# Nine products of ones ahead of the first panels, input tiles in another order, three subtractions moved to VectorE, a copy moved ahead of an exponential, and the last square added by TensorE

## The reference

```
h = rmsnorm(x, norm_attn)
proj = h @ w_in          # queries, keys, values, gates of both mixers
o_nsa = gates over (compressed, selected, sliding-window) attention, 8 heads
o_sb  = stick-breaking attention, 8 heads
mixed = sigmoid(g0) * (o_nsa @ w_up_nsa) + sigmoid(g1) * (o_sb @ w_up_sb)
x = x + mixed @ w_out
x = x + square(relu(rmsnorm(x, norm_mlp) @ w_ff1)) @ w_ff2
return rmsnorm(x, norm_final)
```

## Time and profile before

| | |
|---|---|
| median of 3 runs | 813.46 us (813.44 to 814.03) |
| the profiled execution | 813.46 us, of which the span from first to last instruction is 811.7 us |
| TensorE busy | 786.6 us, 97% of the span |
| VectorE, ScalarE, GpSimd busy | 442.3, 328.7, 283.3 us |
| HBM traffic | 73.90 MB read, 2.13 MB written |

### The profile page before, as it was taken

One profiled execution on the slowest core, in us unless ns is written; L12 is line 12 of the kernel. 1 busy time (PEld: TensorE's weight loads), 2 busy tenths in 40 slices (PEclk: granted clock), 3 DMA queues, 4 the chain that ended last, 5 costly groups with the idle time before them and its releaser, 6 DMA issues.

```text
span 811.7 us, 11300 instructions
## 1 busy us (share of the span) xinstructions
PE 786.6 (97%) x3984; PEld 642.6 (79%) x3984; DVE 442.3 (54%) x780; ACT 328.7 (41%) x583; POOL 283.3 (35%) x123
## 2 busy tenths in 40 slices
PE   6999999999999999999999999999999999999995
PEld 4878988878767677668888888888888888888895
DVE  6545346766646666745736287861177215741354
ACT  6333324488755656556324333232133212321221
POOL 4243333411112212214445254443444444444420
PEclk9999999999999999999999999999999999999998
DMA  7842132210140101024223223223322322233213
GB/s 265 310 140 90 52 129 79 79 52 27 52 130 27 53 27 53 27 78 161 99 103 105 82 100 104 96 85 103 103 88 93 103 103 82 99 103 100 83 52 104
DMA packets 25477, 77.60 MB, mean 96 GB/s; under 512 B 3710, under 2 KB 6966, under 8 KB 25183
## 3 DMA queue, kind: packets, MB, share of 16 engines
q1 hardware_dynamic: 23932, 75.25, 27.8%
q10 hardware_dynamic: 1507, 1.84, 0.8%
HBM read 73.90 MB, written 2.13 MB: 94 GB/s over the span
## 4 chain that ended last, share of the span: by engine, by line
PE 88%; DVE 5%; ACT 3%; DMA 2%; issue 1%; SPq 0%; DVEq 0%; ACTq 0%
PE bank L1166 63%; PE bank L1440 2%; PE bank L1422 2%; PE bank L1359 2%; DMA wraw<-in_panels 2%; PE bank L1473 2%; PE bank L1477 2%; PE bank L1478 2%; PE bank L1371 1%; PE bank L1401 1%; PE bank L1402 1%; PE bank L1184 1%; PE bank L1185 1%; PE bank L1186 1%; PE bank L1266 1%
## 5 line engine op out<-in xcount | busy, mean ns | idle before, releaser
L487 POOL TENSOR_TENSOR wlo<-wraw,whi 128x1024 fp32r<-128x1024 f32 x115 | 275.7, 2400 | 492.6 <-ACT whi L525 246.6
L543 ACT ACTIVATE whi<-wraw 128x1024 fp32r<-128x1024 f32 x48 | 50.9, 1061 | 112.2 <-PE bank L1166 111.2
L1166 PE MATMUL bank<-hh,wlo 128*128 128x512 f32 x304 | 83.1, 398 | 0.6 <-DVE gm L992 0.5
L1166 PE MATMUL bank<-hl,whi 128*128 128x512 f32 x304 | 82.4, 393 | 0.0
L1166 PE MATMUL bank<-hh,whi 128*128 128x512 f32 x304 | 81.4, 392 | 0.0
L1104 DVE TENSOR_TENSOR x_res<-bank,x_res 128x512 f32 (+1 forms) x28 | 19.4, 693 | 107.5 <-PE bank L1166 107.5
L525 ACT ACTIVATE whi<-wraw 128x1024 fp32r<-128x1024 f32 x57 | 59.9, 1052 | 41.7 <-DMA wraw<-in_panels 30.2
L1097 DVE TENSOR_TENSOR tmp<-tmp,rstd_b 128x512 f32<-128x512 f32 x32 | 68.7, 2145 | 1.1
L1166 PE MATMUL bank<-h2h,wlo 128*128 128x512 f32 x256 | 66.0, 391 | 0.0
L1166 PE MATMUL bank<-h2l,whi 128*128 128x512 f32 x256 | 65.5, 389 | 0.0
L1166 PE MATMUL bank<-h2h,whi 128*128 128x512 f32 x256 | 65.5, 389 | 0.0
(11 more groups left out here) (240 smaller groups left out, 1324.0 us busy)
## 6 DMA issues: line engine op xcount, KB each, us to landing
wraw<-in_panels SPq DMA_DIRECT2D x117, 512.0 KB, 3.3
w1k<-in_w SPq DMA_DIRECT2D x1, 2048.0 KB, 9.3
w1v<-in_w SPq DMA_DIRECT2D x1, 2048.0 KB, 14.5
hank<-bias_by_distance SPq DMA_DIRECT2D x4, 512.0 KB, 6.5
x_res<-in_xT SPq DMA_DIRECT2D x4, 512.0 KB, 4.4
out_dram<-x_res SPq DMA_DIRECT2D x16, 128.0 KB, 1.8
xs<-in_xT SPq DMA_DIRECT2D x4, 256.0 KB, 7.0
xs<-in_xT ACTq DMA_DIRECT2D x4, 256.0 KB, 6.6
```

The costliest lines, as they stand in the source:

```text
L487: nc.gpsimd.tensor_tensor(wlo[:, s], wraw[s][:], whi[:, s].bitcast(F32), ALU.subtract).then_inc(w_lo, 1)
L543: A(whi[:, s], wraw[s][:], ACT.Copy).then_inc(w_hi, 1)
L1166: ins = M(b[:, cols], lhs, (xl if a == 1 else xh)[:, row + k, cols], start=(m == 0), stop=(m == 23))
```

## The change

- **Warm.** As soon as the matrix `ones` is set, TensorE does nine products of it by itself, 128 columns each, into a bank that nothing has used yet.
- **Start order.** `xT` lies in memory tile by tile (256 KB in one piece) where a tile was 128 rows of 2 KB at a distance of 16 KB. SyncE's queue starts tiles 1, 3, 5, panel 1, tile 7, panels 2 and 3; ScalarE's queue starts tiles 0, 2, 4, 6. All engines take the tiles in the order `X_ORDER` = 0, 1, 2, 3, 5, 4, 6, 7. ScalarE rounds panel 0's second half after three tiles and panel 1 after six. TensorE does three products for each tile as it comes (rounded, `wlo`, `hl`), then panel 1's products of those six tiles, then both panels' for the last two.
- **Low halves.** VectorE makes the low halves of panels 1, 2 and 3 in place of GpSimd. `sparse_values` does its eight products with `hl` first, and waits for the low halves behind them.
- **Copy ahead.** In each step of the sparse loop ScalarE's copy of unit `i-3` stands ahead of the exponential of unit `i`.
- **End.** The last square is not added to `fin_ss`: TensorE sums `fin_ss` without it, and adds the product of ones by the last square itself. The second half's odd tiles are written out by ScalarE's queue.

The diff, with unchanged lines mostly left out:

```diff
 RING = 4
+X_ORDER = [0, 1, 2, 3, 5, 4, 6, 7]
+X_EARLY = 6
+WARM = 9
...
+        def output(eng, t, n):
+            eng.wait_ge(y_fin, KT * t + n + 1)
+            eng.dma_start(outT[:, n, HALF[t]], x_res[:, n, HALF[t]]).then_inc(out_sem, 16)
...
-            for k in range(0, KT, 2):
-                if k < 4:
-                    sp.dma_start(wraw[0][:, 2 * k:2 * k + 4], panels[0].rearrange("p (k m) -> p k m", k=8)[:, 2 * k:2 * k + 4]).then_inc([first_in, w_in[0]][k // 2], 16)
-                sp.dma_start(xs[:, k, :], xT[:, k, :]).then_inc(x_in[k], 16)
+            def half_panel(i, landed):
+                sp.dma_start(wraw[0][:, 4 * i:4 * i + 4], panels[0].rearrange("p (k m) -> p k m", k=8)[:, 4 * i:4 * i + 4]).then_inc(landed, 16)
+            def input_tile(k):
+                sp.dma_start(xs[:, k, :], xT[k]).then_inc(x_in[k], 16)
+            half_panel(0, first_in)
+            input_tile(1)
+            half_panel(1, w_in[0])
+            input_tile(3)
+            input_tile(5)
             panel(1)
+            input_tile(7)
...
             for n in range(RING):
-                sp.dma_start(x_res[:, 2 * n:2 * n + 2], xT[:, 2 * n:2 * n + 2, :]).then_inc(xres_in, 16)
+                sp.dma_start(x_res[:, 2 * n:2 * n + 2], xT[2 * n:2 * n + 2].rearrange("k p t -> p k t")).then_inc(xres_in, 16)
...
             for t in range(2):
-                for n in range(KT):
-                    sp.wait_ge(y_fin, KT * t + n + 1)
-                    sp.dma_start(outT[:, n, HALF[t]], x_res[:, n, HALF[t]]).then_inc(out_sem, 16)
+                for n in range(0, KT, t + 1):
+                    output(sp, t, n)
...
                 nc.gpsimd.tensor_tensor(wlo[:, 0, half], wraw[0][:, half], whi[:, 0, half].bitcast(F32), ALU.subtract).then_inc(done, 1)
-            low(1)
-            for c in range(2):
-                pool.wait_ge(w_hi, P_V + c + 1)
-                nc.gpsimd.tensor_tensor(vw_l[:, :, P * c:P * c + P], wraw[P_V + c][:], vw_h[:, :, P * c:P * c + P].bitcast(F32), ALU.subtract).then_inc(w_lo, 1)
...
             act.dma_start(nrm[:], norms).then_inc(small_in, 16)
-            for k in range(1, KT, 2):
-                act.dma_start(xs[:, k, :], xT[:, k, :]).then_inc(x_in[k], 16)
+            for k in range(0, KT, 2):
+                act.dma_start(xs[:, k, :], xT[k]).then_inc(x_in[k], 16)
...
-            for k in range(KT):
-                if k < 2:
-                    act.wait_ge([first_in, w_in[0]][k], 16)
-                    A(whi[:, 0, 4 * k:4 * k + 4], wraw[0][:, 4 * k:4 * k + 4], ACT.Copy).then_inc([first_hi, w_hi][k], 1)
-                if k == 0:
-                    act.wait_ge(small_in, 16)
+            def first_half(i, landed, done):
+                act.wait_ge(landed, 16)
+                A(whi[:, 0, 4 * i:4 * i + 4], wraw[0][:, 4 * i:4 * i + 4], ACT.Copy).then_inc(done, 1)
+            first_half(0, first_in, first_hi)
+            act.wait_ge(small_in, 16)
+            for i, k in enumerate(X_ORDER):
+                if i == 3:
+                    first_half(1, w_in[0], w_hi)
+                if i == X_EARLY:
+                    split(1)
...
                 A(hh[:, k], xs[:, k], ACT.Copy, scale=nrm[:, 0, k:k + 1]).then_inc(h_hi, 1)
-            split(1)
...
                     stick_out_high(PAIRS - 1)
+                u = i - 3
+                if 0 <= u < UNITS:
+                    r, run = unit(u)[3:]
+                    ps = result(act, ("t", u))
+                    if run >= 4 and run % 2 == 0 and r == 0:
+                        sparse_pv_done(act, run - 4)
+                    emptied(A(probs_tile(run, r),
+                              ps[:, 0:P * (r + 1)].rearrange("p (k t) -> p k t", k=r + 1), ACT.Copy), ("t", u))
...
                     split_half(P_GM + GM_SB + RING + (i - 5) // 6, i % 6 % 5)
-                u = i - 3
-                if 0 <= u < UNITS:
-                    r, run = unit(u)[3:]
-                    ps = result(act, ("t", u))
-                    if run >= 4 and run % 2 == 0 and r == 0:
-                        sparse_pv_done(act, run - 4)
-                    emptied(A(probs_tile(run, r),
-                              ps[:, 0:P * (r + 1)].rearrange("p (k t) -> p k t", k=r + 1), ACT.Copy), ("t", u))
...
                 A(tmp[:, 0, c], tmp[:, 0, c], ACT.Exp, scale=-0.5).then_inc(rs3, 1)
+            for n in range(1, KT, 2):
+                output(act, 1, n)
...
             dve.wait_ge(small_in, 16)
-            for k in range(KT):
-                dve.wait_ge(h_hi, k + 1)
+            for i, k in enumerate(X_ORDER):
+                dve.wait_ge(h_hi, i + 1)
...
                                        op0=ALU.mult, op1=ALU.subtract).then_inc(h_lo, 1)
+            dve.wait_ge(w_lo, 1)
+            dve.wait_ge(w_hi, 2)
+            V.tensor_tensor(wlo[:, 1], wraw[1][:], whi[:, 1].bitcast(F32), ALU.subtract).then_inc(w_lo, 1)
+            for c in range(2):
+                dve.wait_ge(w_hi, P_V + c + 1)
+                V.tensor_tensor(vw_l[:, :, P * c:P * c + P], wraw[P_V + c][:], vw_h[:, :, P * c:P * c + P].bitcast(F32), ALU.subtract).then_inc(w_lo, 1)
...
                     emptied(V.tensor_tensor(x_res[:, 4 + n, c], ps[:, c], x_res[:, 4 + n, c], ALU.add), ("end", t, n))
-                    add_sq(4 + 4 * t + n, fin_sq[:, n % 2, c], fin_ss[:, c], y_sq, y_ss)
+                    if (t, n) != (1, 3):
+                        add_sq(4 + 4 * t + n, fin_sq[:, n % 2, c], fin_ss[:, c], y_sq, y_ss)
...
+            pe_.wait_ge(set_done, 1)
+            for i in range(WARM):
+                M(bank[7][:, 0:P], ones[:], ones[:], start=True, stop=True)
...
-            for k in range(KT):
+            def rounded(i):
+                k = X_ORDER[i]
...
-                pe_.wait_ge(h_hi, k + 1)
-                M(b0[:], whi[:, 0, k, :], hh[:, k, :], start=(k == 0), stop=False)
-                if k:
-                    pe_.wait_ge([first_lo, w_lo][(k - 1) // 4], 1)
-                    M(b0[:], wlo[:, 0, k - 1, :], hh[:, k - 1, :], start=False, stop=False)
-            M(b0[:], wlo[:, 0, KT - 1, :], hh[:, KT - 1, :], start=False, stop=False).then_inc(w_used, 1)
+                pe_.wait_ge(h_hi, i + 1)
+                M(b0[:], whi[:, 0, k, :], hh[:, k, :], start=(i == 0), stop=False)
+            def weight_low(i):
+                k = X_ORDER[i]
+                pe_.wait_ge([first_lo, w_lo][k // 4], 1)
+                return M(b0[:], wlo[:, 0, k, :], hh[:, k, :], start=False, stop=False)
+            def input_low(i):
+                pe_.wait_ge(h_lo, i + 1)
+                return M(b0[:], whi[:, 0, X_ORDER[i], :], hl[:, X_ORDER[i], :], start=False, stop=(i == KT - 1))
+            def second_rounded(i):
+                pe_.wait_ge(h_hi, i + 1)
+                M(b1[:], whi[:, 1, X_ORDER[i], :], hh[:, X_ORDER[i], :], start=(i == 0), stop=False)
+            def second_input_low(i):
+                pe_.wait_ge(h_lo, i + 1)
+                return M(b1[:], whi[:, 1, X_ORDER[i], :], hl[:, X_ORDER[i], :], start=False, stop=(i == KT - 1))
+            for i in range(X_EARLY):
+                rounded(i)
+                if i >= 1:
+                    weight_low(i - 1)
+                if i >= 2:
+                    input_low(i - 2)
+            weight_low(X_EARLY - 1)
+            input_low(X_EARLY - 2)
+            input_low(X_EARLY - 1)
...
-            for k in range(KT):
-                M(b1[:], whi[:, 1, k, :], hh[:, k, :], start=(k == 0), stop=False)
-            for k in range(KT):
-                pe_.wait_ge(h_lo, k + 1)
-                ins = M(b0[:], whi[:, 0, k, :], hl[:, k, :], start=False, stop=(k == KT - 1))
+            for i in range(X_EARLY):
+                second_rounded(i)
+            for i in range(X_EARLY - 1):
+                second_input_low(i)
+            for i in range(X_EARLY, KT):
+                rounded(i)
+                second_rounded(i)
+                ins = weight_low(i)
+            ins.then_inc(w_used, 1)
+            second_input_low(X_EARLY - 1)
+            for i in range(X_EARLY, KT):
+                ins = input_low(i)
...
-            for k in range(KT - 1):
-                M(b1[:], whi[:, 1, k, :], hl[:, k, :], start=False, stop=False)
+            for i in range(X_EARLY, KT - 1):
+                second_input_low(i)
...
-            filled(M(b1[:], whi[:, 1, KT - 1, :], hl[:, KT - 1, :], start=False, stop=True), ("pan", 1))
+            filled(second_input_low(KT - 1), ("pan", 1))
...
+                o = claim(pe_, ("v", r))[:, 0:VW]
+                pe_.wait_ge(gn_split, 1)
+                pe_.wait_ge(w_hi, P_V + 2)
+                rows = slice(P * r, P * r + P)
+                for k in range(KT):
+                    M(o, hl[:, k, rows], vw_h[:, k, :], start=(k == 0), stop=False)
...
-                o = claim(pe_, ("v", r))[:, 0:VW]
...
-                    xh, xl = hh[:, k, P * r:P * r + P], hl[:, k, P * r:P * r + P]
-                    low = M(o, xh, vw_l[:, k, :], start=(k == 0), stop=False)
```

(19 more changed lines are left out.)

## The result

The changed kernel takes 809.43 us (median of 8 runs, 808.19 to 813.05) where the kernel before takes 813.95 (8 runs, 813.44 to 814.88): ratio 0.9945, 95% interval 0.9931 to 0.9959, a gain of 4.52 us between the medians. The profiled execution took 808.81 us, its span is 807.0 where that of the kernel before is 811.7.

A forecast was written before the change was run, and what follows sets the result against it. TensorE, busy 97% of the span, was taken as the bound. Gains of 2.4 (start), 3.5 (loop) and 0.95 us (end) sum to 6.85: 813.46 - 6.85 = 806.6 us, range 804.3 to 809.6 with rivals.

The forecast's parts named there:

- Rival 1: Start: TensorE's clock comes up no earlier and the start gives only 0.5 us; time 808.5 us, chance 0.12.
- Rival 2: Sparse loop: the copy ahead buys nothing, since turns then wait for VectorE's normalisation; time 810.1 us, chance 0.08.
- The data and the order, 1.9 us: Start: earlier data and three products per tile let the values begin at 19.9 us in place of 21.83.
- The new layout: Start: one-piece tiles cure slow packets between 4 and 6 us; 0.5 us taken, nothing if the cause is another.
- The products of ones cost nothing: Start: the nine products end between 3.4 and 5.8 us, hidden in TensorE's first wait of 6.5 us.
- A shift at the start is handed on to the end: Whole kernel: later stages hang on TensorE by semaphores, so the start's 2.4 us would reach the end.
- Low halves on VectorE: Start: each takes 1.3 us on VectorE; sums of squares ready 0.4 us before use; no term in the sum.
- rival 4: Start: sums of squares late by more than the margin, behind three subtractions; time 807.8 to 809 us, chance 0.08.
- The copy ahead, 3.5: Sparse loop: the copy fits ScalarE's idle time before the exponential, saving TensorE 3.5 us, range 1.5 to 5.
- Rival 3: Sparse loop: the copy holds the exponential back, making the kernel slower; 826.1 us at half the units, chance 0.02.
- The end, 0.95: End: 0.45 us from the last square's add leaving the chain, 0.5 from two output queues; 0.45 if transfers bind.
- The one turn that the forecast worked out by itself: Sparse loop, turn at 242.45 us: 1.3 to 1.4 of its 1.70 us wait for ScalarE's copy would be saved.

The follow-up runs named there:

- e6: The change with TensorE's transposes of the distance rows (dts) and VectorE's copy of their result moved behind the hidden projection; 809.22 us, ratio 0.9935.
- e10: The change with GpSimd's low halves written in two instructions and ScalarE's probability copy back behind the exponential; 808.90 us, ratio 0.9931.
- e11: The change with GpSimd's low halves in two instructions and the distance-row transposes behind the hidden projection; 803.57 us, ratio 0.9866.
- e13: e12 with the old order of the first two panels' products and panel 1 rounded behind all eight tiles; 804.65 us, ratio 0.9881.
- e15: e12 with x's rows 16 KB apart in DRAM again, as in the kernel before; 804.18 us, ratio 0.9871.
- e1: The change without the nine products of ones ahead of the first panels; 809.14 us, ratio 0.9937.
- e16: e12 with the low halves of panels 1 to 3 made by GpSimd again; 804.34 us, ratio 0.9876.
- e12: e11 with more products of ones on TensorE, ahead of the first, third and fifth tiles, to fill idle spells; 803.76 us, ratio 0.9874.
- the halves: Edit that writes each GpSimd low half in two instructions of half the elements; added alone to the change, 804.77 us, ratio 0.9890.

## Why the prediction held, and where its terms were off

It gave 806.6 us with 804.3 to 809.6; measured were 809.4. The direction held; of the sum of 6.85, 4.66 came. That the range held is partly luck. The forecast's own range, from the ends of its terms, was 804.5 to 808.5 and missed; only the part added for the rivals reached to 809.6, and four of the change's eight runs lie above that. Part of the shortfall came by what rivals 1 and 2 describe, but 0.82 us came by a wait that no rival had.

One of its signs of being wrong appeared. It named "as many waits for VectorE as they had for ScalarE" in the loop's turns: the change has five waits for VectorE, 4.1 us, where the kernel before had three for ScalarE, 2.3. Another sign, the values after 21 us, didn't appear in the profiled execution, but did in e6, e10 and e11, whose start is the same. The loop became 2.35 us shorter, not the 3 to 4 that it gave.

1. **The data and the order, 1.9 us: right in the number**, 1.94 measured, with 30 x 0.227 behind the first 18 products and no wait for the last tile. But it had the 30 begin when panel 1 is rounded, at 13.1. Panel 1 was rounded at 12.4, and what they waited for were the 18 products, until 13.08 (12.9 forecast). That the two came out within 0.1 us is chance. With the clock up early the order alone is worth 1.17 (e13).
2. **The new layout, 0.5 on top: mis-sized in this sum.** It did bring data sooner: panel 1 landed at 11.3 and not 12.0, and 4 to 6 us moved 312 GB/s for 251. But the end of the start is a chain through tile 5, rounded at 10.8, and the nine products from there to 13.08. In e15 the layout is worth 0.35 to 0.65, so it is part of the 1.94 and the order less than 1.9 of it. I had added two gains that shorten one chain.
3. **The products of ones cost nothing: right.** They end at 5.27, the first data product starts at 6.25. That they bring the clock up is not shown (e1); the rise came at 10.0 us in the profiled execution and at 11 to 14.6 in others. Rival 1 is thus true of some executions, with values up to 1.8 us later than 19.89, which probably is what lifts the median above the profiled 808.8. The Trainium skill's page "TensorE: Matmul & The Clock Gate" ("What's actually happening") has the moment of the rise differ between runs; the traces agree, with 10.0 to 14.6 us. I cited that and gave the rival 0.12 as if the clock were one or the other.
4. **"A shift at the start is handed on to the end": wrong**, the step that failed most plainly. 0.82 us were lost where TensorE waits for `dts`. In the kernel before, this transfer was no wait in any row, as it had landed 0.81 us ahead of its use; the start moved by 1.94 and the landing by 0.40. I looked for waits and not for margins. e6 gives it back.
5. **Low halves on VectorE: right in kind.** 1.18 each (1.3 taken), the margin of `sqs` 2.0 and not 0.4, so rival 4 did not come. The move is worth 0.82 us, which the forecast had not priced (e16).
6. **The copy ahead, 3.5: its worth was right and its cover wrong.** Where the normalisation is on time it is worth 3.78 (e10). In the change 2.35 came, since "other timing may add one or take one away" was no luck but a mechanism: GpSimd's 2.4 us hold a normalisation in turns that come sooner. Rival 2 was half true. Rival 3, the copy holding exponentials back, is refuted by the shorter loop.
7. **The end, 0.95: 1.12 measured**, 0.54 for the sum of ones and 0.58 behind it. Transfers didn't bind, since 1.8 us follow the last issue in both kernels; the issue pace of 0.47 did.

The one turn that the forecast worked out by itself came as it said. Of its wait 0.3 us were to be left, behind the half panel and unit 3's copy; in the change 0.35 are left (ScalarE, then TensorE):

```profile
240.87 0.58 ACT L703 ACTIVATE pt<-bank 128x512 f32<-128x512 f32 x1
...
241.50 0.44 PE L1485 MATMUL bank<-ident,ns 128*128 128x128 f32 x2 [0.35 <-ACT pt L703]
```

The forecast's 242.2, when that turn is due, stands in no row; it fits 240.75 plus a step of 1.45.

The seven runs beside the profiled one reach from 808.19 to 813.05. The highest had a mean granted clock of 0.991 in place of 0.997; that it is the start's clock alone is likely and not shown, as it has no trace.

The best kernels are e11 and e12, at 803.6 and 803.8 us: 1.3% under the kernel before, some 10 us, of which 4.7 are the halves and 0.8 to 1.3 the moved rows.

## What to carry to other kernels

When two engines exclude each other, it is the longest instruction of the one that nobody waits for that hurts: write it in pieces, even if the pieces cost more in sum (2.7 for 2.4 us here bought 4.7). Before adding gains of two edits, ask whether both shorten the same chain, and which wait is just behind the one that goes. A gain at the start must be followed past every transfer whose issue or landing doesn't move with it; look for those that arrive less ahead of their use than the gain is long, which no list of waits shows.

## What the runs showed that was not expected

- VectorE gets the shared access between two GpSimd instructions that stand back to back: normalisations beside GpSimd took at most 1.52 us in place of 2.60.
- The read of 220 KB for `dts`, issued when the 32 KB that it reads had been written to DRAM, took from its issue to its last semaphore step 6.4 us in the kernel before and 7.4 to 9.5 in the other thirteen executions.
- The clock's upper level was lost during the start after idle spells of 0.7 to 1.1 us, in five executions of the twelve that have products of ones; in e12, e13 and e16 it was kept with idle spells of at most 0.5, and in e13 with one of 0.99 at 6.4 us. So the length of an idle spell alone doesn't decide it.
- The column of the granted clock reads 1.00 ahead of 10 us in the change, where products of 512 columns start 0.43 us apart.
